# Expert weight pieces as one 8 KB run per partition, with transposes that pick every fourth and every second column

## The reference

```python
def expert_block(args):
    xblk, e = args
    hdn = jax.nn.silu(xblk @ w_gate_e[e]) * (xblk @ w_up_e[e])
    return hdn @ w_down_e[e]
```

## Time and profile before

| | |
|---|---|
| timed runs | 2605.37, 2606.14, 2608.58 us, median 2606.14 |
| span of the profiled execution | 2603.9 us, 37119 instructions |
| PE busy | 2195.3 us (84%) |
| DVE, ACT busy | 1345.1 us (52%), 1137.2 us (44%) |
| mean granted TensorE clock | 0.934 of full speed |
| moved by DMA | 351.27 MB, mean 135 GB/s |
| chain that ended last | the gathers of `combine` behind the experts |

### The profile page before, as it was taken

One profiled execution on the slowest core, in us unless ns is written; L12 is line 12 of the kernel. 1 busy time (PEld: TensorE's weight loads), 2 busy tenths in 40 slices (PEclk: granted clock), 3 DMA queues, 4 the chain that ended last, 5 costly groups with the idle time before them and its releaser, 6 DMA issues. The chain is left out here.

```text
span 2603.9 us, 37119 instructions
## 1 busy us (share of the span) xinstructions
PE 2195.3 (84%) x11260; PEld 1771.6 (68%) x11260; DVE 1345.1 (52%) x1570; ACT 1137.2 (44%) x1545; POOL 228.7 (9%) x297
## 2 busy tenths in 40 slices
PE   4469898888989897699999979978928999999991
PEld 2357675666667664599988869977825777777770
DVE  5323545545354544411255552213246888888884
ACT  3223444534444342311156642113205777777770
POOL 0210202102020210000000000000000011010003
PEclk9779999999999997899999989998958999999995
DMA  2310302112030110311222331132127999999986
GB/s 89 68 33 10 84 24 59 33 51 74 9 83 25 43 31 29 110 49 40 58 85 86 93 120 49 40 106 78 41 108 276 380 394 399 394 396 396 394 327 231
DMA packets 199072, 351.27 MB, mean 135 GB/s; under 512 B 19852, under 2 KB 127544, under 8 KB 198920
## 3 DMA queue, kind: packets, MB, share of 16 engines
q1 hardware_dynamic: 181544, 293.55, 31.7%
q0 software_dynamic: 13872, 44.35, 5.5%
q10 hardware_dynamic: 3584, 12.58, 1.2%
HBM read 301.87 MB, written 48.58 MB: 135 GB/s over the span
## 5 line engine op out<-in xcount | busy, mean ns | idle before, releaser
L2238 DVE TENSOR_TENSOR e_w_lo<-e_raw,e_w_hi 128x2048 fp32r<-128x2048 f32 x192 | 434.4, 2289 | 91.6 <-ACT e_w_hi L2165 74.4
L2165 ACT CAST e_w_hi<-e_raw 128x2048 fp32r<-128x2048 f32 x192 | 365.9, 1908 | 62.5 <-PE e_y_ps L103 35.9
L101 PE MATMUL proj_ps<-w_qkv_hi,xh 128*128 128x384 f32 x544 | 232.0, 427 | 24.9 <-PEq L286 19.1
L101 PE MATMUL ux_ps<-xh,r_wx_hi 128*128 128x364 f32 x576 | 192.1, 333 | 20.2 <-DVE r_wx_lo L765 16.7
L102 PE MATMUL ux_ps<-xl,r_wx_hi 128*128 128x364 f32 x576 | 191.1, 332 | 0.0
L103 PE MATMUL ux_ps<-xh,r_wx_lo 128*128 128x364 f32 x576 | 190.8, 331 | 0.0
L102 PE MATMUL proj_ps<-w_qkv_lo,xh 128*128 128x384 f32 x544 | 186.2, 342 | 0.0
L103 PE MATMUL proj_ps<-w_qkv_hi,xl 128*128 128x384 f32 x544 | 186.1, 342 | 0.0
L1185 PE MATMUL out_ps<-mT 128*128 128x512 f32 (+3 forms) x384 | 169.8, 525 | 3.7 <-DVEq L84 2.9
L101 PEld LDWEIGHTS proj_ps<-w_qkv_hi,xh 128*128 128x128 f32 x544 | 106.0, 195 | 52.1 <-issue 45.4
L1384 ACT ACTIVATE mT<-st_ps 128x512 f32<-128x512 f32 x192 | 93.6, 488 | 100.7 <-PE st_ps L1170 45.8
(11 more groups left out here) (406 smaller groups left out, 5120.2 us busy)
## 6 DMA issues: line engine op xcount, KB each, us to landing
e_raw<-w_gate_e SPq DMA_DIRECT2D x64, 1024.0 KB, 9.0
e_raw<-w_up_e SPq DMA_DIRECT2D x64, 1024.0 KB, 9.5
e_raw<-w_down_e SPq DMA_DIRECT2D x64, 1024.0 KB, 10.0
w_raw<-w_in SPq DMA_DIRECT2D x24, 512.0 KB, 4.6
r_wx<-w_in SPq DMA_DIRECT2D x24, 512.0 KB, 3.8
slot_y<-e_y ACTq DMA_DIRECT2D x32, 384.0 KB, 6.1
slot_y<-zrows POOLq DMA_DIRECT2D x24, 352.0 KB, 4.2
mT<-cache_k SPq DMA_DIRECT2D x8, 1024.0 KB, 5.6
```

Of the source, the lines that this page charges most:

```text
L101: nc.tensor.matmul(out, a_hi, b_hi, start=start, stop=False)
L2165: sc.copy(w_hi[u][:, :], w.raw[c][:, :]).then_inc(wh_ready, 1)
L2238: v.tensor_tensor(w_lo[u][:, :], w.raw[c][:, :], w_hi[u][:, :], ALU.subtract).then_inc(wl_ready, 1)
```

## The change: the layout of a piece and the columns of the transposes

A partition of each piece is now one run of 8 KB in memory: four neighbouring rows of 512 floats for gate and up, two neighbouring rows of 1024 floats for down. The load's destination is the whole tile without a split in two. To match, the k-th transpose of four in `turn_x` takes columns k, k+4, k+8 and so on of its 512 columns, and the f-th of two in `turn_h` takes columns f, f+2, f+4 and so on of its 256. No instruction is added, removed or put in another place on any engine; the numbers of matmuls, of loads and of bytes stay.

```diff
     def load(self, sp, g, c, e):
 
-        half = slice(c % 2 * 2, c % 2 * 2 + 2)
-        if c < 4:
-            w = (g.w_gate_e, g.w_up_e)[c // 2]
-            src = w[0, bass.ds(e, 1)].rearrange("o (a p b) n -> p (o a) (b n)", p=P, b=2)[:, half, :]
-        else:
-            src = g.w_down_e[0, bass.ds(e, 1)].rearrange("o (a p) n -> p (o a) n", p=P)[:, half, :]
-        sp.dma_start(self.raw[c][:, :].rearrange("p (a n) -> p a n", a=2), src).then_inc(self.loaded[c], 16)
+        half, b = c % 2, 4 if c < 4 else 2
+        w = (g.w_gate_e, g.w_up_e, g.w_down_e)[c // 2]
+        src = w[0, bass.ds(e, 1)].rearrange("o (a p b) n -> p (o a) (b n)", p=P, b=b)[:, half, :]
+        sp.dma_start(self.raw[c][:, :], src).then_inc(self.loaded[c], 16)
@@
                     for k in range(KT):
-                        wide = xb[:, k // 2 * 2 * P:(k // 2 + 1) * 2 * P].rearrange("c (q b) -> c b q", b=2)
-                        last = te.transpose(xT_ps[:, k // 4, (k % 4) * CAP:(k % 4 + 1) * CAP], wide[:, k % 2, :], g.ident[0:CAP, 0:CAP])
+                        wide = xb[:, k // 4 * BANK:(k // 4 + 1) * BANK].rearrange("c (q b) -> c b q", b=4)
+                        last = te.transpose(xT_ps[:, k // 4, (k % 4) * CAP:(k % 4 + 1) * CAP], wide[:, k % 4, :], g.ident[0:CAP, 0:CAP])
@@
                     for f in range(FT):
-                        last = te.transpose(hT_ps[:, f * CAP:(f + 1) * CAP], h_sb[:, f * P:(f + 1) * P], g.ident[0:CAP, 0:CAP])
+                        wide = h_sb[:, f // 2 * 2 * P:(f // 2 + 1) * 2 * P].rearrange("c (q b) -> c b q", b=2)
+                        last = te.transpose(hT_ps[:, f * CAP:(f + 1) * CAP], wide[:, f % 2, :], g.ident[0:CAP, 0:CAP])
```

## The result

The changed kernel takes 2610.36 us (median of 20 runs, 2607.87 to 2614.49) against 2604.62 us for the kernel before (20 runs, 2602.87 to 2608.77). The ratio is 1.0018, with a 95% interval of 1.0012 to 1.0024: 3.1 to 6.3 us slower. (The two medians differ by 5.7 us.) The prediction took any difference under 0.2%, 5.2 us, for no change: the ratio lies just under that, its interval reaches past it and leaves out zero. The time is far from the 2638 us that was forecast. It is nearly that of the first rival, 2610.3 us, and in part by luck: the rival added 4.2 us to the median of three runs, 2606.14 us, and the median of the 20 runs above is 1.5 us lower.

The account below looks back on a forecast made before the run. PE was taken to bound the kernel, with DMA full but hidden. 31 x (0.135 + 0.89) = 31.8 us took the profiled 2603.9 to 2635.7, plus 2.2 for the median: 2638 us, 1.2% slower; range 2608 to 2646 us.

Parts of the forecast that it names:

- the first rival: `e_x` transposes: every fourth column costs what every second does, only `e_h` pays 4.2 us; 2610.3 us, chance 0.20.
- What bounds the kernel: Middle of the expert loop: PE sets the 17.93 us block; DMA is also full but hidden, with 2.5 us of room.
- The loads at nothing: Weight loads in 8 KB runs: best case 0.5 us of a block's DMA work, counted as zero because PE hides it.
- The straight line: SP's queue: transfer cost of 38.4 ns per 1000 bytes plus 9 ns per packet, so 8 KB runs save 3% at best.
- The transposes of `e_h`: `turn_h` on PE: going from neighbouring to every second column costs 4 x 34 ns = 0.135 us a block.
- The transposes of `e_x`: `turn_x` on PE: every fourth column instead of second, priced by bytes spanned, costs 0.89 us a block.
- The count of 31: Turns of `e_x` and `e_h` taken to lie on the path: 31 of 33 and 31 of 32.
- The flat price: `e_x` weight loads: step four costs the same as step two, total 2610.3 us; chance 0.20.
- point of decision: `e_x` weight loads: over 4 ns longer at step four than at step two carries the total past 0.2%.
- A faster early part: Early stall behind ACT's store issue: fewer packets may end it, up to 5 us back; chance of over 0.2% faster 0.05.
- Slower transfers: 8 KB runs hold an engine longer; DMA 3% slower would give 2617 us with a flat price; chance 0.05.
- the lower bound: Tail, last two down loads where PE idles: -0.2 us allowed for longer runs, while the forecast itself took zero.

Follow-up runs that it names:

- e1: Kernel before with all six loads in 8 KB runs, transposes left as they were: 2606.99 us, ratio 1.0004 to the kernel before.
- e4: Kernel before with all loads in 8 KB runs and all twelve transposes of a block on neighbouring columns: 2599.29 us, ratio 0.9967.
- e6: Kernel before, 4 KB runs kept, with GpSimd copying the token block so `e_x` transposes read neighbouring columns: 2603.06 us, ratio 0.9986.
- e12: Changed kernel with VectorE writing tokens (in the merge) and hidden block sorted, no GpSimd copy: 2598.21 us, ratio 0.9972 to the kernel before.
- e3: Kernel before with only gate and up in 8 KB runs and `turn_x` at step four: 2606.37 us, ratio 1.0002.
- e9: Changed kernel with the transposes of `e_x` at step eight (32 bytes) instead of four: 2608.85 us, one run.
- e8: Changed kernel with VectorE writing the hidden block sorted, so `e_h` transposes read neighbouring columns: 2606.95 us, ratio 1.0002 to the kernel before.

## Why the prediction was wrong

- **What bounds the kernel** was read rightly: PE's block of 17.93 us, with DMA full but hidden. e1 (loads alone: no change) and e4 (transposes cheaper: 8 us less) show both halves. The gapless 494.00 us and the landing times that did not grow were the rows that told it.
- **The loads at nothing** held. The straight line gave 3% for 8 KB as the best case; the transfers of a block go from 17.87 or 17.97 us (before, e6) to 17.7 or 17.8 (e4, e12), about 1%, and the queue's time for the same bytes falls by 1.6% (e1).
- **The transposes of `e_h`**: mechanism and size held. 0.135 us a block was forecast, 0.12 measured around them and 0.11 in the block. The loads take 208 ns and not quite 217, and a transpose costs 0.11 / 4 = 28 ns more instead of 34. The count of 31 with 0.11 gives 3.4 us instead of 4.2.
- **The transposes of `e_x`** is the step that failed. I took "the price follows the bytes that the load spans", 0.89 us a block or 27.6 us, "over zero because both measured steps fit a price per byte spanned, and a flat price fits only one of them". The runs put 0.00 to 0.01 us there (e3), and e9 shows the price even a little lower at step eight. The argument was weak. The measured steps did not fit a price per byte as they stood, since the span doubled and the price rose 2.4 times. And of steps one and two, step one is the case without gaps. A flat price for all steps, with another rate for neighbours, fits two points as well as a line does, and a slope can't be read from one point on each side of such a change of kind. The measured steps gave no reason to choose, and I put 0.57 on one side.
- **The Trainium skill's rule**, on SBUF — State Buffer, "Door 1: The DMA port swizzle", that each access which goes on to a new line of 16 bytes pays: no run bears it out for TensorE's loads, since two columns in a line cost what one does (217 and 218 ns). Nor does its "4 fp32" for free, since step two already costs 77 ns.
- **The rivals.** The flat price, with a chance of 0.20, is what happened: its point of decision (4 ns a load) is not reached in the changed kernel, 1 ns. In e3 the loads do take 6 ns more, and the block still only 0.01 us. That the time came out within 0.1 us of its 2610.3 is luck, as said above: 3.4 us and not 4.2 are the transposes'. A faster early part did not come: ACT's issue of the store, which I thought the transfers might hold up, took 5.07 us, where the earlier trace rows has 4.78.

```profile
2002.53 5.07 ACTq L2186 DMA_DIRECT2D slot_y<-e_y  x1
```

- Slower transfers did not come either (e1). In the tail the last casts wait 5.35 and 0.58 us for their loads, against 5.71 and 0.61. That is 0.4 us less, where the lower bound had 0.2, and in one profile of each.
- **What stays open** is why a load with gaps costs 77 ns more than one without, whatever the step, and why it is 204 ns at step eight and 223 in e3 and e8 where the changed kernel has 218. Open too is how GpSimd's copy makes PE's block longer, and what makes the stretches ahead of the loop, around the early stall and behind the loop differ by up to 5 us from profile to profile.

## What to carry to other kernels

A transpose on TensorE that reads its fp32 operand with a step costs about the same here at steps two, four and eight, so a layout may as well take the longest run of memory that the step can buy; but the first step away from neighbouring columns is paid in full (0.11 / 4 = 28 to 0.26 / 8 = 33 ns for each transpose here), and where PE sets the period it is the whole effect. Find what sets the period before valuing longer runs: here they were worth nothing until PE's block was shortened, and then, by e4 and e12 against e6, they were most likely what kept it short. Where an operand is written by VectorE anyway, sort it in that write rather than in a copy of GpSimd's.

## What was unexpected of the hardware

- TensorE's weight load of 128 fp32 columns for a transpose: 140 ns for neighbours, 207 to 217, 218 to 223 and 204 ns at steps of 8, 16 and 32 bytes.
- GpSimd's copy of 96 x 1024 fp32 takes 2372 ns reading at 8 bytes and 2999 ns at 16, and beside the latter VectorE's subtraction of 128 x 2048 goes from 2290 to between 2299 and 2325 ns in the mean.
- VectorE's write of 96 x 512 in scattered order takes 1107 ns instead of 678, and of 128 x 1024 in two halves 2.30 us instead of 1.28.
